# First recurrent units on the raw residual, and an earlier copy out of the first query unit

## The chip, the cores and the metric

The kernel runs on one core of one Trainium2 chip. The metric is the device time of one execution in microseconds, the median of the runs shown. Engines are named TensorE (PE; PEld is its weight load), VectorE (DVE), ScalarE (ACT), GpSimd (POOL) and SyncE (SP, which only issues DMAs). Hi and lo below are the two parts into which a float32 value is split, so that a product is made of three matmuls: hi with hi, hi with lo, lo with hi.

## The reference, cut to what matters

One inference step of a hybrid layer on 1024 prompt positions and 8 sample positions (1032 columns in all) with 1024 channels:

```python
xn = rmsnorm(x, norm_mix)
lru_x, lru_g, q, k, v = split(xn @ w_in)
xc = causal_conv(x_ext, w_conv, b_conv)          # width 4, over lru_x
hs, h_T = rg_lru(xc, ...)                        # gates, then h = a * h + u along the positions
y_lru = (hs * gelu(lru_g)) @ w_branch_lru
q = rmsnorm(q, q_gain); k = rmsnorm(k, k_gain)   # per head of 64 channels
...                                              # attention in three groups, merge, w_o, SwiGLU
```

`rmsnorm(x)` is `x * gain / rms`, with one rms for each position. So a product with the normed input is the product with `x * gain`, each column of which is multiplied by 1/rms afterwards.

## The kernel before, in words

Channels lie on the 128 partitions, in 8 tiles, and positions along the free axis, in 3 chunks of 344. A unit is the product of one 128-channel column of a weight matrix with all 8 input tiles: 3 chunks by 8 tiles by 3 matmuls, 72 matmuls, into one of two halves ("slots") of the PSUM tensor `ups`. The units come in the order of `stream` (line 160): 2 pairs of value units `v`, 8 pairs `lru` (slot 0 the recurrent input, slot 1 its gelu gate), 12 pairs `qk`, then attention and the rest. For each unit SyncE loads the weights, GpSimd splits them (`split`, lines 450 to 457: a cast, then a subtraction) once the unit before in that slot is done, TensorE multiplies, and ScalarE copies the result out of PSUM and so frees the slot (`ps_free`).

Nothing is planned by a program: each engine has its own hand-written list, and semaphores tie them. These parts bear on the change:

- *Start.* ScalarE casts each raw tile `x * gain` to its hi part (`big2`, line 882) and squares it (883). VectorE makes the lo part (1218) and adds up the squares (1222); GpSimd adds two of them (469, 472). TensorE first makes three lines of attention biases (510), which VectorE copies (1213, 1215), and then the first value pair tile by tile on the raw parts (`raw_tile`, 521). Behind its tile 7 come the sums of squares (527), the roots on ScalarE (891) and the reciprocals on VectorE (1227): 1/rms, `rinv`. The value units are scaled by it after their copy out (1232).
- *Normed input.* For tile k: VectorE multiplies by gain and `rinv` (`normed`, 1235), ScalarE casts the hi part of `big1` (910), and the lo part is made by VectorE (1240) or, for tiles 1, 4 and 7, by GpSimd (463). The first `lru` unit waits for each lo part (`normed_ready`, 569); all later units need `big1` too.
- *Recurrence.* For unit i: copy out of PSUM (`front`, 942) with the first tap of the convolution (946, 947), three more taps and three small ones on VectorE (`conv`, 1292 and 1295), two gate products on TensorE for each chunk (`gates`, 566), sigmoids on ScalarE (952, 953), gelu (960), then decay (967, 969), VectorE's squares (1303, 1304), ScalarE's root (971), VectorE's product, scan, small instructions, gelu product and its two parts (`recur`, 1303 to 1316).
- *Query and key units.* ScalarE copies a unit out, squares it and casts the squares (`evac`, 1000 to 1005); VectorE makes their lo part (`square_low`, 1334); TensorE sums the squares of each head in `aux` (`stats`, 590); ScalarE takes the root (1015), VectorE the reciprocal (1339) and the normed unit (1341), which ScalarE stores. `square_low` of the next unit stands behind 1341 in VectorE's list. TensorE runs `stats` of a unit between chunks 1 and 2 of the next one. Ahead of the first `evac` ScalarE waits until the last recurrence is over and issues two output DMAs (985 to 987).

Of the kernel before, what the change touches and what calls it, by code (L numbers as in the profile page):

```python
# [92 lines left out]
def build(nc, A, O):  # L93

    with ExitStack() as ctx:
# [36 lines left out]
        lamt = sout.rearrange("p a n -> p (a n)")[:, 0:4 * KT].rearrange("p (a n) -> p a n", a=4)  # L132
# [3 lines left out]
        sums, odd_sums, rinv = x_sq[:, 0, :], x_sq[:, 1, :], ext[:, 0, 0:NT]  # L136
        fsums, frms = ext[:, 0, 0:NT], ext[:, 3, 0:NT]
        POOL_LOW = (1, 4, 7)
# [55 lines left out]
        nf_done, nhi_done, nlo_dve, nlo_pool = sem("nf_done"), sem("nhi_done"), sem("nlo_dve"), sem("nlo_pool")  # L194
        gmix_ld, xhi_done, xlo_done, odd_done, sum_done = (sem(n) for n in ("gmix_ld", "xhi_done", "xlo_done", "odd_done", "sum_done"))
        vm_done = sem("vm_done")
# [16 lines left out]
        v_stored = two("v_stored")  # L213
# [48 lines left out]
        VO = [ext[:, 2 + j, 0:NT] for j in range(2)]  # L262
# [39 lines left out]

        def wait_low(eng, k):

            if k in POOL_LOW:
                eng.wait_ge(nlo_pool, POOL_LOW.index(k) + 1)
            else:
                eng.wait_ge(nlo_dve, k + 1 - sum(n < k for n in POOL_LOW))

# [20 lines left out]
        def _(sp):  # L330
            for name, iters, nk, src, f0, f1, step, k0 in stream:
# [57 lines left out]
                if name == "v":  # L389
                    first = 1  # L390
                    weights(0, 0)
                    for k in range(KT):
                        sp.dma_start(tmp(k), A["x_T"][k]).then_inc(x_loaded[k], 16)
                        if k == 1:
                            weights(0, 1)
                    for dst, con in consts:
                        sp.dma_start(dst, con).then_inc(const_ld, 16)
                if name == "att0":
# [3 lines left out]
                    for j in range(2):  # L402
                        sp.wait_ge(v_stored[j], 16 * 2)
# [41 lines left out]
        def _(pool):  # L445
# [13 lines left out]
            for name, iters, nk, *_ in stream:  # L459
                first = 0  # L460
                def low(k):
                    pool.wait_ge(nhi_done, k + 1)
                    nc.gpsimd.tensor_tensor(big1[:, 1, k, :], tmp(k), big1[:, 0, k, :].bitcast(F32), ALU.subtract).then_inc(nlo_pool, 1)  # L463

                if name == "v":
                    split(name, nk, 0, 0)
                    split(name, nk, 0, 1)
                    pool.wait_ge(nsq_done, 5)
                    nc.gpsimd.tensor_tensor(odd_sums, odd_sums, x_sq[:, 4, :], ALU.add).then_inc(odd_done, 1)
                    pool.wait_ge(nsq_done, 8)  # L470
                    pool.wait_ge(odd_done, 1)
                    nc.gpsimd.tensor_tensor(odd_sums, odd_sums, x_sq[:, 7, :], ALU.add).then_inc(odd_done, 1)
                    split(name, nk, 1, 0)
                    split(name, nk, 1, 1)
                    low(POOL_LOW[0])
                    continue
                if name == "lru":
                    first = 1
                    split(name, nk, 0, 0)
                    low(POOL_LOW[1])  # L480
                    low(POOL_LOW[2])
                    split(name, nk, 0, 1)
# [6 lines left out]
        def _(pe):  # L489
# [22 lines left out]
            pe.wait_ge(lines_ld, 48)  # L512
            bias_line(0)
            bias_line(1).then_inc(u_ps, 1)
            pe.wait_ge(u_sb, 1)
            bias_line(2).then_inc(u_ps, 1)

            def raw_tile(slot, k):
                for c in range(NCH):
                    for w, a in ((0, 0), (0, 1), (1, 0)):  # L520
                        ins = nc.tensor.matmul(ups[:, slot, c, 0:CH], wsp[:, slot, w, k, :], big2[:, a, k, c * CH:(c + 1) * CH],  # L521
# [8 lines left out]
            for n in range(KT + LEAD):  # L530
                if n < KT:
# [4 lines left out]
                    raw_tile(0, n)  # L536
# [9 lines left out]
                if n >= LEAD:  # L546
# [3 lines left out]
                    raw_tile(1, n - LEAD)  # L550
# [18 lines left out]
            def normed_ready(c, k):  # L569
                if c == 0:  # L570
                    wait_low(pe, k)
# [21 lines left out]
            def qk(i, first):  # L593
                for j in range(2):
                    if first and j == 0:
                        for c in range(2):
                            unit("qk", i, j, big1, parts=(c,))
                            gates(KT - 1, c + 1)
                        pe.wait_ge(gate_ev, KT * NCH + 1)
                    else:  # L600
                        unit("qk", i, j, big1, parts=(0, 1))
                    if j:
                        stats(0, i)
                    elif not first:
                        stats(1, i - 1)
# [4 lines left out]
            qk(0, True)  # L610
            with pe.Fori(1, 12) as i:
                qk(i, False)
# [242 lines left out]
        def _(act):  # L855
# [19 lines left out]
            act.dma_start(gmix[:], A["c_norm_mix"]).then_inc(gmix_ld, 16)  # L875
            act.dma_start(lines.rearrange("p (g n) -> p g n", g=NG), A["c_lines"].rearrange("g b n -> b g n")).then_inc(lines_ld, 16)
            act.dma_start(relx[0:NBK, :], A["rel_bias"]).then_inc(lines_ld, 16)
            act.dma_start(relx[NBK:NBK + 1, :], A["c_one"]).then_inc(lines_ld, 16)
            act.wait_ge(gmix_ld, 16)
            for k in range(KT):  # L880
# [3 lines left out]
                if k == 2:  # L884
                    act.wait_ge(u_sb, 2)
                    act.dma_start(u_s.rearrange("(g h) n -> h g n", g=NG), u_lines).then_inc(u_stored, 16)
            act.wait_ge(bd_zero, 1)
            gate_weights(0)
            for c in range(NCH):
# [5 lines left out]
            def values_out(n):  # L895
                i, j = n // 2, n % 2
                act.wait_ge(unit_done[j], i + (T0["v"] + 2))
                if i:
                    act.wait_ge(v_stored[j], 16)
                nc.scalar.activation(chunks(VO[j]), ups_v[j], ACT.Copy).then_inc(ps_free[j], 1)  # L900

            def values_store(n):
                j = n % 2
                act.wait_ge(vm_done, n + 1)
                nc.scalar.activation(sqkv[:, 24 + n, :], VO[j][:, SEQ:NT], ACT.Copy).then_inc(sqc_done, 1)
                act.dma_start(qkv_s[24 + n], VO[j][:, 0:SEQ]).then_inc(v_stored[j], 16)

# [8 lines left out]
            for k in range(4):  # L916
                normed_hi(k)
            values_out(2)
            for k in range(4, KT):
                normed_hi(k)  # L920
            values_store(2)

            act.wait_ge(lam_dve, 1)
            nc.scalar.activation(lamt[:, 1, :], lamt[:, 0, :], ACT.Exp, scale=-1.0).then_inc(lam_act, 1)
            act.wait_ge(lam_dve, 2)
            nc.scalar.activation(lamt[:, 3, :], lamt[:, 2, :], ACT.Ln).then_inc(lam_act, 1)


            values_out(3)
            values_store(3)  # L930
# [6 lines left out]

            def front(i):
# [4 lines left out]
                act.wait_ge(ps_free[0], i + (T0["lru"] + 2))  # L943
                act.wait_ge(u_done, i + 1)
                apart(act)
                nc.scalar.activation(XC[:, 0:SEQ], LX[:, 0:SEQ], ACT.Identity, bias=col(i, 4), scale=col(i, 0))
                nc.scalar.activation(XC[:, SEQ:NT], LX[:, SEQ + 3:NT + 3], ACT.Identity, bias=col(i, 4), scale=col(i, 3)).then_inc(xc0_done, 1)
# [25 lines left out]
            front(0)  # L973
# [702 lines left out]
```

## Time and profile before

| what | value |
|---|---|
| median of 3 runs | 2086.37 us (2084.69 to 2089.06) |
| the profiled execution's own time | 2086.76 us |
| its span, first to last instruction | 2085.0 us |
| mean granted TensorE clock | 0.988 of full speed |
| TensorE busy | 2020.2 us, 97% of the span |
| VectorE, ScalarE, GpSimd busy | 44%, 24%, 27% |

Times in the rows are microseconds from the span's start. A row of the timeline has start, duration, engine, line, instruction, output and inputs, and how many instructions in a row it merges; in brackets stands how long the engine was idle before and what released it. The ends of matmuls are modelled. A row of the waits says who waited for whom: total, how often, and the longest. L501 is a unit's matmul wherever it is called from.

### The profile page before, as it was taken

How to read it: one execution, taken by the hardware profiler on the slowest of the kernel's cores; microseconds unless marked ns; L12 is line 12 of the kernel's file. 1: busy time of each engine (PE TensorE's matmuls, PEld its weight loads, DVE VectorE, ACT ScalarE, POOL GpSimd, SP SyncE). 2: the span in 40 equal slices, each digit the busy share in tenths (PEclk: the TensorE clock that was granted, in tenths of full speed). 3: DMA queues.
4: the chain of work that ended last, by engine and by line, in shares of the span. 5: the costliest groups of instructions: out<-in, count | busy, mean ns of one | idle time of the engine just before them, and what ended most of it. 6: DMA issues, size and time to landing. Idle time of an engine off the chain costs nothing.

```text
span 2085.0 us, 32283 instructions
## 1 busy us (share of the span) xinstructions
PE 2020.2 (97%) x12884; PEld 1955.8 (94%) x12884; DVE 907.1 (44%) x913; ACT 509.4 (24%) x725; POOL 562.0 (27%) x330
## 2 busy tenths in 40 slices
PE   7899989999989999999989899999999999999999
PEld 7899988999979999999978899999999999999999
DVE  6666666767763232222256464443220333203331
ACT  4366653333334333233311012201100000000000
POOL 3433322222321111111122133233232332323322
PEclk9999999999999999999999999999999999999999
DMA  5211111222233333424377352111111111111112
GB/s 201 93 35 42 43 42 53 98 83 80 80 126 123 125 106 112 132 101 139 109 267 256 125 196 106 41 51 40 50 41 50 50 40 50 41 50 51 40 57 85
DMA packets 71594, 188.42 MB, mean 90 GB/s; under 512 B 9314, under 2 KB 28797, under 8 KB 70781
## 3 DMA queue, kind: packets, MB, share of 16 engines
q1 hardware_dynamic: 41312, 136.97, 19.3%
q10 hardware_dynamic: 30236, 50.82, 6.7%
q8 instruction: 32, 0.52, 0.1%
q14 instruction: 14, 0.11, 0.0%
HBM read 145.09 MB, written 45.81 MB: 92 GB/s over the span
## 4 chain that ended last, share of the span: by engine, by line
PE 89%; DVE 6%; ACT 1%; issue 1%; DMA 1%; POOL 1%; ACTq 0%; SPq 0%; DVEq 0%; POOLq 0%
PE ups L501 64%; PE ups L627 12%; PE ups L652 3%; PE ups L677 3%; PE aux L664 2%; PE aux L566 1%; PE aux L590 1%; PE ups L521 1%; DVE x L1339 1%; PE aux L641 0%; DVE x L1494 0%; ACT x L1085 0%; DVE ext L1227 0%; POOL big L463 0%; DVE x L1309 0%
## 5 line engine op out<-in xcount | busy, mean ns | idle before, releaser
L501 PE MATMUL ups<-big,wsp 128*128 128x344 f32 x9216 | 1482.4, 322 | 19.2 <-POOL wsp L457 8.5
L501 PEld LDWEIGHTS ups<-big,wsp 128*128 128x128 f32 x9216 | 1462.8, 189 | 35.8 <-issue 16.8
L455 POOL CAST wsp<-wraw 128x1024 fp32r<-128x1024 f32 (+2 forms) x160 | 163.6, 1022 | 1465.9 <-issue 725.2
L457 POOL TENSOR_TENSOR wsp<-wraw,wsp 128x1024 fp32r<-128x1024 f32 (+2 forms) x160 | 382.5, 2391 | 12.8
L627 PE MATMUL ups<-big,wsp 128*128 128x344 f32 x1728 | 291.8, 324 | 0.0
L627 PEld LDWEIGHTS ups<-big,wsp 128*128 128x128 f32 x1728 | 272.7, 189 | 5.3 <-issue 5.2
L1339 DVE RECIPROCAL x<-x 128x1024 f32<-128x1024 f32 x24 | 157.3, 6553 | 75.8 <-ACT x L1015 75.8
L1377 DVE SCALAR_TENSOR_TENSOR x<-ups,ext 128x256 f32<-128x256 f32 (+1 forms) x96 | 48.0, 542 | 235.8 <-PE aux L664 147.2
L1190 ACT ACTIVATE ext<-ext 128x1032 f32<-128x1032 f32 x22 | 23.5, 1068 | 482.5 <-DVE ext L1594 482.4
L1596 DVE TENSOR_TENSOR ext<-ups,ext 128x1032 f32<-128x1032 f32 x22 | 27.1, 1234 | 215.4 <-PE ups L501 215.4
L1610 DVE TENSOR_TENSOR x<-ups,x 128x1032 f32 x24 | 29.6, 1233 | 203.7 <-PE ups L501 203.7
L1085 ACT ACTIVATE x<-x,ext 128x128 f32<-128x128 f32 (+1 forms) x192 | 70.9, 440 | 60.2 <-DVE ext L1385 59.9
L1599 DVE TENSOR_TENSOR ext<-ext 128x1032 f32<-128x1032 f32 x22 | 71.1, 3233 | 4.8 <-DVE ext L1596 4.8
L1594 DVE TENSOR_TENSOR ext<-ups,ext 128x1032 f32<-128x1032 f32 x22 | 27.1, 1234 | 105.4 <-PE ups L501 105.1
L652 PE MATMUL ups<-ext 64*128 64x128 f32 (+1 forms) x384 | 67.1, 476 | 4.7 <-DVEq L1362 4.7
L677 PE MATMUL ups<-x 128*128 128x65 f32 x560 | 67.8, 270 | 0.0
L677 PEld LDWEIGHTS ups<-x 128*128 128x128 f32 x560 | 66.8, 192 | 0.0
L652 PEld LDWEIGHTS ups<-ext 64*128 64x128 f32 x384 | 43.5, 281 | 14.6 <-issue 13.1
L1015 ACT ACTIVATE x<-aux,epst 128x1024 f32<-128x1024 f32 x24 | 26.8, 1117 | 121.2 <-PE aux L590 121.2
L1390 DVE COPY x<-ups 128x260 f32<-128x260 f32 x48 | 20.4, 425 | 81.3 <-PE ups L677 81.3
L1075 ACT ACTIVATE x<-aux 128x768 f32<-128x768 f32 (+1 forms) x32 | 28.6, 892 | 82.9 <-PE ups L677 67.3
L1383 DVE TENSOR_REDUCE x<-x 128x2 f32<-128x256 f32 (+1 forms) x96 | 47.6, 539 | 1.7
(189 smaller groups left out, 1165.4 us busy)
## 6 DMA issues: line engine op xcount, KB each, us to landing
wraw<-w_in SPq DMA_DIRECT2D x52, 512.0 KB, 3.5
wraw<-w_ffn_in SPq DMA_DIRECT2D x44, 512.0 KB, 3.2
out_qkv<-x ACTq DMA_DIRECT2D x28, 512.0 KB, 2.7
ext<-out_qkv SPq DMA_DIRECT2D x24, 512.0 KB, 4.4
x<-x_T SPq DMA_DIRECT2D x16, 516.0 KB, 8.2
x<-gate_s SPq DMA_DIRECT2D x16, 516.0 KB, 4.2
wraw<-w_merge SPq DMA_DIRECT2D x16, 512.0 KB, 5.1
wraw<-w_ffn_out SPq DMA_DIRECT2D x16, 512.0 KB, 3.5
```

The lines of the kernel that those rows point to most:

```text
L455: nc.gpsimd.tensor_copy(hi, raw).then_inc(w_hi, 1)
L457: nc.gpsimd.tensor_tensor(lo, raw, hi.bitcast(F32), ALU.subtract).then_inc(w_split[slot], 1)
L501: ins = nc.tensor.matmul(ups[:, slot, c, 0:CH], wsp[:, slot, w, k, :], src[:, a, k, c * CH:(c + 1) * CH], start=(k == 0 and w + a == 0), s ...
L627: ins = nc.tensor.matmul(ups[:, 0, c, 0:CH], wsp[:, slot, w, k, :], big1[:, a2, k, c * CH:(c + 1) * CH], start=(k == 0 and w + a2 == 0), s ...
L652: ins = nc.tensor.matmul(s_bank[:, hh, 256 * m + 256 - P * nk:256 * m + 256], toks(QT, g, b)[hr], toks(KTT, g, b, nk)[hr], start=True, sto ...
L664: ins = nc.tensor.transpose(pt_bank[:, hh, c:c + P], SB[:, hh, c:c + P], ident[:])
L677: ins = nc.tensor.matmul(o_bank[:, at:at + HD + 1], PTS[:, hh, c:c + P], VTOK[:, b + 1 - nk + k, hh, :], start=(k == 0), stop=(k == nk - 1))
L1085: ins = nc.scalar.activation(SB[:, hh, cols], SB[:, hh, cols], ACT.Exp, bias=NM[:, 2 * m + hh:2 * m + hh + 1])
L1339: step.step(nc.vector.reciprocal(rms_t, rms_t))
L1377: ins = nc.vector.scalar_tensor_tensor(SB[:, :, cols], s_bank[:, :, cols], SCALE, BT[:, :, 0:P * nk][:, :, ::-1], ALU.mult, ALU.add)
L1383: ins = nc.vector.tensor_reduce(OT[:, 2 * n + m, :, HD + 1], SB[:, :, cols], AX_X, ALU.max)
L1599: step.step(nc.vector.tensor_tensor(ext[:, 1, 0:NT], ext[:, 0, 0:NT], ext[:, 1, 0:NT], ALU.mult))
```

## The change

- The first `lru` pair multiplies the raw parts in `big2`, without waiting for the normed input. At the exit VectorE multiplies both results by `rinv`, out of PSUM: the recurrent input into `LX0` in place of ScalarE's copy, the gate into `GE` ahead of the gelu. Before the second `lru` unit TensorE waits for all eight lo parts of the normed input (`nlo_done`).
- All lo parts of the normed input and all sums of squares are VectorE's; GpSimd only splits weights. The norm of tiles 6 and 7 moves behind the exit of the first unit, around its convolution. Value units 2 and 3 are scaled and stored behind the first gates.
- At the start TensorE's bias lines move between the raw tiles and are copied by ScalarE; SyncE loads the gain vector first; ScalarE runs one dummy activation early; the softplus chain of the decay constants moves ahead of the reciprocals.
- ScalarE's first `evac` waits only for the last gate product on VectorE instead of the whole recurrence; `square_low(0, 0)` goes into the last recurrence, ahead of the gelu product. The two output DMAs follow `evac(0, 0)`, still behind the recurrence's end. TensorE's first statistics move from the second to the third query unit, the next two sets to one and two chunks of the fourth; from the third pair on the order is the old one.

The core of the diff:

```diff
                 if name == "v":
                     first = 1
+                    sp.dma_start(gmix[:], A["c_norm_mix"]).then_inc(gmix_ld, 16)
                     weights(0, 0)
...
-            unit("lru", 0, 0, big1, ready=normed_ready)
-            unit("lru", 0, 1, big1)
+            unit("lru", 0, 0, big2)
+            unit("lru", 0, 1, big2)
             gates(0, 0)
+            pe.wait_ge(nlo_done, KT)
...
-            qk(0, True)
-            with pe.Fori(1, 12) as i:
-                qk(i, False)
+            for c in range(2):
+                unit("qk", 0, 0, big1, parts=(c,))
+                gates(KT - 1, c + 1)
+            unit("qk", 0, 0, big1, parts=(2,))
+            unit("qk", 0, 1, big1)
+            pe.wait_ge(gate_ev, KT * NCH + 1)
+            unit("qk", 1, 0, big1, parts=(0,))
+            stats(0, 0)
+            unit("qk", 1, 0, big1, parts=(1, 2))
+            unit("qk", 1, 1, big1, parts=(0,))
+            stats(1, 0)
+            unit("qk", 1, 1, big1, parts=(1,))
+            stats(0, 1)
+            unit("qk", 1, 1, big1, parts=(2,))
+            with pe.Fori(2, 12) as i:
+                qk(i)
...
+            act.wait_ge(ones_done, 1)
+            nc.scalar.activation(st[:, 0:1], epst[:], ACT.Identity, scale=epst[:])
             act.wait_ge(gmix_ld, 16)
...
+            act.wait_ge(const_ld, CONSTS)
+            act.wait_ge(nlo_done, 1)
+            tap(0, ext[:, 1, :])
+            for k in range(6, KT):
+                normed_hi(k)
+            act.wait_ge(nlo_done, 4)
             gate(0, 0)
+            gate(0, 1)
+            act.wait_ge(ps_free[1], T0["lru"] + 2)
+            nc.scalar.activation(GE, GE, ACT.Gelu_apprx_tanh)
+            gate(0, 2)
+            values_store(2)
+            values_store(3)
+            gate_weights(1)
+            act.wait_ge(gx_done, 1)
+            front(1)
+            decay(0)
+            gate(1, 0)
...
+            act.wait_ge(u_done, KT + 1)
+            evac(0, 0)
+            act.wait_ge(lru_done, KT)
+            act.dma_start(O["lru_out"], sout[:]).then_inc(out_done, 16)
+            act.dma_start(O["state_out"], stc[:]).then_inc(out_done, 16)
+            root(0, 0)
+            evac(0, 1)
...
                 nc.vector.tensor_copy(sout[:, ds(i, 1), 11:20], H[:, SEQ - 1:NT])
+                if last:
+                    square_low(0, 0)
                 step.step(nc.vector.tensor_tensor(U, H, GE, ALU.mult))
...
+            for k in range(6):
+                normed(k)
+                if k:
+                    normed_low(k - 1)
+            normed_low(5)
+            LX0 = ext[:, 1, :]
+            step.step(nc.vector.memset(LX0[:, 0:3], 0.0))
+            dve.wait_ge(unit_done[0], T0["lru"] + 2)
+            nc.vector.tensor_tensor(chunks(LX0[:, 3:3 + NT]), ups_v[0], chunks(rinv), ALU.mult).then_inc(ps_free[0], 1)
+            normed(6)
+            conv(0, LX0)
+            normed(7)
+            normed_low(6)
+            normed_low(7)
...
+            dve.wait_ge(unit_done[1], T0["lru"] + 2)
+            nc.vector.tensor_tensor(chunks(GE), ups_v[1], chunks(rinv), ALU.mult).then_inc(ps_free[1], 1)
+            values_scaled(2)
+            values_scaled(3)
```

## Rows read from the trace of the kernel before

**Rows 1.** The waits of TensorE, the two at the last recurrence.

```profile
PE aux L590 <- DVE ext_r L1334: 12.6, 2, 9.9
PE ups L501 <- ACT x L953: 2.7, 1, 2.7
```

**Rows 2.** TensorE's timeline, start to the first gates.

```profile
14.69 20.64 PE L521 MATMUL ups<-big,wsp 128*128 128x344 f32 x117 [1.93 <-DVE big L1218]
...
41.14 24.72 PE L501 MATMUL ups<-big,wsp 128*128 128x344 f32 x156
...
76.28 21.54 PE L501 MATMUL ups<-big,wsp 128*128 128x344 f32 x123 [2.13 <-POOL big L463]
```

**Rows 3.** TensorE's timeline, last recurrence to the third statistics.

```profile
290.36 1.32 PE L566 MATMUL aux<-x,bd 128*128 128x344 f32 x4
294.34 13.13 PE L501 MATMUL ups<-big,wsp 128*128 128x344 f32 x72 [2.67 <-ACT x L953]
317.40 2.07 PE L590 MATMUL aux<-ext_r,bones_r 128*128 128x512 f32 x4 [9.92 <-DVE ext_r L1334]
...
344.50 1.09 PE L590 MATMUL aux<-ext_r,bones_r 128*128 128x512 f32 x4
```

**Rows 4.** One microsecond: length, TensorE busy (instructions), granted clock, DMA share, GB/s.

```profile
296.00:297.00 1.00, 1.00 (x5) 0.50 0.00 0
```

**Rows 5.** Timeline of the first 17 us; one row lists line 882's instructions.

```profile
0.76 0.43 ACTq L875 DMA_DIRECT2D gmix<-c_norm_mix  x1
...
6.20 2.34 POOL L457 TENSOR_TENSOR wsp<-wraw,wsp 128x1024 fp32r<-128x1024 f32 x1
...
6.91 1.28 ACT L882 ACT_TABLE_LOAD   x1 [6.91 <-DMA x<-x_T]
...
7.55 2.73 PE L510 MATMUL aux<-big_f 33*8 33x384 f32 x4 [7.55 <-DMA big_f<-c_one]
...
9.53 1.04 POOL L455 CAST wsp<-wraw 128x1024 fp32r<-128x1024 f32 x1 [0.99 <-DMA wraw<-w_in]
...
13.27 3.68 DVE L1218 SCALAR_TENSOR_TENSOR big<-x,gmix,big 128x1032 fp32r<-128x1032 f32 x3
...
L882 ACT ACTIVATE big<-x,gmix x8: 1138/1141/1155, 8.2 to 22.2; 128x1032 fp32r<-128x1032 f32 x8
```

**Rows 6.** Timeline: VectorE and GpSimd at once, both in SBUF, and with PSUM.

```profile
58.15 3.27 POOL L457 TENSOR_TENSOR wsp<-wraw,wsp 128x1024 fp32r<-128x1024 f32 x1
59.08 3.43 DVE L1240 TENSOR_TENSOR big<-x,big 128x1032 fp32r<-128x1032 f32 x1
...
1502.42 1.04 POOL L455 CAST wsp<-wraw 128x1024 fp32r<-128x1024 f32 x1 [7.84 <-PE ups L501]
1502.42 1.23 DVE L1594 TENSOR_TENSOR ext<-ups,ext 128x1032 f32<-128x1032 f32 x1 [4.43 <-PE ups L501]
```

**Rows 7.** Timeline: tap and convolution of the first recurrent unit.

```profile
87.70 1.24 ACT L946 ACTIVATE x<-ext,par 128x1024 f32<-128x1024 f32 x1
...
89.27 4.64 DVE L1292 SCALAR_TENSOR_TENSOR x<-ext,par,x 128x1024 f32<-128x1024 f32 x3 [3.93 <-ACT x L947]
...
94.61 0.17 DVE L1299 COPY sout<-ext 128x11 f32<-128x11 f32 x1
```

**Rows 8.** Timeline of ScalarE and VectorE from the last recurrence on.

```profile
300.71 1.07 ACT L971 ACTIVATE x<-x 128x1032 f32<-128x1032 f32 x1 [1.27 <-DVE x L1304]
...
305.17 2.29 DVE L1309 TENSOR_TENSOR_SCAN x<-x 128x1024 f32<-128x1024 f32 x1
...
311.40 0.34 ACTq L986 DMA_DIRECT2D out_lru_out<-sout  x1
...
312.88 1.03 ACT L1000 ACTIVATE x<-ups 128x1032 f32<-128x1032 f32 x1 [11.11 <-issue]
...
319.51 1.11 ACT L1015 ACTIVATE x<-aux,epst 128x1024 f32<-128x1024 f32 x1 [3.32 <-PE aux L590]
...
329.54 1.21 DVE L1334 TENSOR_TENSOR ext_r<-x,ext_r 128x1024 fp32r<-128x1024 f32 x1
```

More of the change, by code:

```diff
@@ L212, in build @@
         sqc_done = sem("sqc_done")
-        v_stored = two("v_stored")
+        v_stored = [sem(f"v_stored{n}") for n in range(4)]
         bt_fill = sem("bt_fill")
@@ L591, in stats, with qk @@
                 ins.then_inc(st_done[j], 1)
-            def qk(i, first):
+            def qk(i):
                 for j in range(2):
[L595 to L605, printed above, removed]
+                    unit("qk", i, j, big1, parts=(0, 1))
+                    stats(1 - j, i - 1 + j)
                     unit("qk", i, j, big1, parts=(2,))
@@ L936, in col, with tap @@
                 return par[:, ds(i, 1), n]
+            def tap(i, lx):
+                act.wait_ge(ps_free[0], i + (T0["lru"] + 2))
+                act.wait_ge(u_done, i + 1)
+                apart(act)
+                nc.scalar.activation(XC[:, 0:SEQ], lx[:, 0:SEQ], ACT.Identity, bias=col(i, 4), scale=col(i, 0))
+                nc.scalar.activation(XC[:, SEQ:NT], lx[:, SEQ + 3:NT + 3], ACT.Identity, bias=col(i, 4), scale=col(i, 3)).then_inc(xc0_done, 1)
             def front(i):
@@ L942, in front @@
                 nc.scalar.activation(chunks(LX[:, 3:3 + NT]), ups_v[0], ACT.Copy).then_inc(ps_free[0], 1)
[L943 to L947, printed above, removed]
+                tap(i, LX)
             def gate(i, c):
@@ L1016, in root @@
                     .then_inc(rt_done[j], 1)
-            def qk(i, first):
-                if not first:
-                    root(i - 1, 1)
+            act.wait_ge(u_done, KT + 1)
[5 more added lines that the diff above has]
+            evac(0, 1)
+            with act.Fori(1, 12) as i:
+                root(i - 1, 1)
                 evac(i, 0)
-                if not first:
-                    store(i - 1, 0)
+                store(i - 1, 0)
                 root(i, 0)
                 evac(i, 1)
-                if not first:
-                    store(i - 1, 1)
-            qk(0, True)
-            with act.Fori(1, 12) as i:
-                qk(i, False)
+                store(i - 1, 1)
             root(11, 1)
@@ L1219, in _ @@
                                                ALU.mult, ALU.subtract).then_inc(xlo_done, 1)
-                if k > 1 and k not in POOL_LOW:
+                if k:
                     dve.wait_ge(nsq_done, k + 1)
-                    step.step(nc.vector.tensor_tensor(sums, sums, x_sq[:, k, :], ALU.add))
-            dve.wait_ge(odd_done, 2)
-            nc.vector.tensor_tensor(sums, sums, odd_sums, ALU.add).then_inc(sum_done, 1)
-            for c in range(NCH):
-                dve.wait_ge(nrt_done, c + 1)
-                step.step(nc.vector.reciprocal(part(rinv, c), part(rinv, c)))
```

204 lines of the change are left out of this document (84 added, 120 removed).

## The prediction, made before the changed kernel ran

> **What bounds the kernel now.** I read the busy shares first: TensorE is busy in 97% of the span, so only two things can shorten the time: TensorE's waits, and stretches in which it works at half clock. The waits by line come next, kept here to the two at the last recurrence: 9.9 us on the squares of the first query unit and 2.7 us on a sigmoid of ScalarE [rows 1]. Then TensorE's own timeline. Its 117 matmuls on the raw residual begin only at 14.69 and take 20.64 us; 156 run at 158 ns each (24.72 us); after that the first recurrent unit comes in handfuls of three, and 123 matmuls resume at 76.28 [rows 2]. 288 matmuls from 41.14 at that pace would end at 86.8; they end at 97.82. So 11.0 us are lost there. At the end of the recurrence the two waits stand inside matmul groups that are themselves stretched: 72 matmuls take 13.13 us against 11.4 [rows 3]. The clock tells why: from 296 to 297, right after the wait of 2.67 us, the granted clock is 0.50, the 1.2 GHz level, with TensorE busy [rows 4]. I count 1.7 us for each such stretch.
>
> **Part 1, the start.** Now the first cast waits for x at 6.91 and then for a table load of 1.28, and the bias lines stand ahead of everything [rows 5]. The early dummy activation takes the table load out. The gain vector's load moves ahead of weights and x on SP, so both come later by its issue of 0.4 [rows 5]; on ScalarE's queue it frees as much for the bias lines, which nobody waits for early any more. So the casts start at 7.3, and ScalarE delivers one every 2.0 us (8 from 8.2 to 22.2) [rows 5], the first at 8.45.
>
> VectorE and GpSimd exclude each other here. A 1.23 us subtraction that asked at 59.08, while GpSimd's subtraction ran to 61.42, took 3.43: it waited for the other's end. At 1502.42 a VectorE product out of PSUM and a GpSimd cast began together and both ran at full speed [rows 6]. The Trainium skill, page "SBUF — State Buffer", section "Who interferes with whom", says that an instruction with two SBUF inputs and a GpSimd one that reads SBUF block each other for the whole instruction; the rows agree. It speaks against this change, which brings VectorE's work forward into GpSimd's first two splits; without blocking the sum would be 2.1 us better.
>
> By the rows: the first split, 0.4 later, ends at 8.95, so the first low part runs 8.95 to 10.15, and TensorE starts at 10.15 instead of 14.69. The second split's cast (1.04) follows to 11.2, the second low part to 12.4, GpSimd's subtraction (2.34) to 14.75, VectorE's new second sum to 16.0, the third low part to 17.2, each VectorE step at 1.23 [rows 5]. TensorE has two tiles, 18 matmuls, 2.85 us, plus the 2.1 that its slow first matmuls cost before (20.64 against 117 times 0.158 [rows 2]): done at 15.1, idle to 17.2. Then 99 matmuls (15.65) and the three bias lines, six instructions at about 0.34 (four took 2.73 on an engine that had just begun [rows 5], and I take half; 2.05 in all): 34.9, where it was 35.33. **Gain 0.4.** Bounds: 2.5 if the blocking does not starve it; a loss of 1.3 if the pause adds a half-clock stretch. I take the middle, since the blocking is what the nearest rows show. The two sums that move from GpSimd to VectorE are in these steps. Casting the bias lines on ScalarE, softplus before the reciprocals and the later store of the bias rows hide behind TensorE's 13 tiles; uncovered they would cost some 1 to 3 us.
>
> **Part 2, the first recurrent units.** They read what the value units read, so TensorE runs 288 matmuls from 40.7 without a wait and reaches the gates at 86.35 instead of 97.82, and ends their 1.3 us [rows 3] at 87.65. Behind that stands a new wait: all eight low parts of the normed input, with the whole of the next unit queued behind it on TensorE. The first unit ends at 40.7 + 34.25 = 74.95. VectorE scales it out of PSUM (1.23 [rows 6], not blocked) to 76.2. ScalarE's tap takes 1.57 (87.70 to 89.27 [rows 7]): 77.8. Meanwhile the norm of tile 6 asked at 76.2 and is blocked by the split of 75.0 to 78.45: done 79.7. The convolution took 5.3, of which 0.9 was a block [rows 7]: 84.1, before the gates need it. Norm of tile 7, low part 6: 86.6. The split that the second unit's end at 86.35 releases puts its cast in between (87.7), then low part 7: 88.9. **TensorE waits 1.3 us.** Bounds: nothing if VectorE goes first and the splits come late, 2.5 if the subtraction too gets in front. Three low parts moved from GpSimd cost VectorE 3.7, hidden: by the same steps it is through with tiles 0 to 5 near 71 and then idles until 74.95. The second unit's scaling, the two value products and the four gate-weight DMAs, ahead of ScalarE's next copy out, have until that unit's end near 102 to be done; they come to less than 6 us after the gates. Sum of both parts: the next unit starts at 88.9 instead of 99.1: **10.2 us.**
>
> **Part 3, the last recurrence** (clock of the run before). TensorE no longer waits at 291.67 [rows 3]: 24 matmuls to 295.5, 72 to 306.9, 24 to 310.7; there the first statistics stand now. The copy out is behind ScalarE's root at 300.71 [rows 8] and takes 4.5 less 1.2 (312.88 to 317.40 [rows 3, 8]), so it is done by 306. VectorE's scan ends near 306.2 (2.29 [rows 8]; the split that blocks the product ahead of it has moved to 295.5). The inserted subtraction asks at 306.9, just as the second query unit releases a split: cast to 307.9, subtraction to 309.1, on time for 310.7. But what follows it, a product and two copies, 3.2 us (3.9 from the scan's end to the next output DMA [rows 8], less 0.7 that I count for four small instructions), then meets GpSimd's subtraction and ends at 314.7, 3.3 later than before (311.40 [rows 8]). ScalarE waits for exactly that before its two output DMAs (about 0.9) and the first root, 315.6. From root to the next low part took 11.24, of which 0.9 was a block [rows 8]: 10.4 free, so 326.0. TensorE is there at 323.1, waits 2.9, and the third statistics follow after only 24 matmuls: ready 327.0 + 10.5 = 337.5, TensorE there at 330.9, **a wait of 6.6 us that is new**. Before they ran at 344.50 [rows 3]. 7.0 earlier, less a half-clock stretch as after the old 9.9 us wait (1.0 on the statistics, 1.7 on 72 matmuls [rows 3]): **4.3 us gained**. Bounds: 9.5 if VectorE is not blocked and the clock holds; nothing if two more blocks of 2 us fall into the chain.
>
> **Sum.** 10.2 + 4.3 = 14.5 us off the profiled execution's 2086.76 (span 2085.0), 2072.3. The median of the runs is 0.4 lower, so 2071.9. After the third statistics the order of work is the old one, so the rest only moves forward; the later store of values 2 and 3 has until the attention.
>
> **Rivals.** *The waits stay short* (0.25): blocking falls the other way in all three places: 2.1 + 1.3 + 5.2 more, 2063.3. For: whoever asks first wins, and the instants are within 0.1 us. Against: GpSimd's 3.4 us must be served somewhere.
> *Each short wait also costs half clock* (0.12): the pauses of 2.1 and 1.3 each bring a stretch of 1.7, 2075.3, and up to 2077.5 with the longer one. For: rows 4 after 2.67 us. Against: these waits are shorter. The Trainium skill, page "TensorE: Matmul & The Clock Gate", section "HAM oscillation — how this bites in real kernels", describes waits between groups that leave each next group cold.
> *The early copy buys nothing* (0.08): the statistics of the query loop are a chain through root, reciprocal and subtraction; with two more blocks the third set still runs at 344.50. Only part 2 is left: 2076.2, with the second rival's half clocks 2079.6.
> *The change does not do it* (0.03): some wait of mine on the first units is a longer one, the normed input then being late by the whole 10 us; within 0.2%.
> *Slower* (0.03): in the query loop the chain has 12.3 us per unit (11.4 of matmuls, about 0.9 of statistics) and uses 10.4. If the shifted start put GpSimd's subtraction on the product and subtraction after the reciprocal, instead of under the reciprocal, chain 10.4 + 2.3 plus the blocked copy 0.6 would be 13.3: 22 statistics, each 1 us late, 22 us against 14.5: 2094. It decides from a chain of 12.3 on. Against: splits follow unit ends, and these keep their places in the loop.
> My forecast itself holds 0.49.
>
> **How the numbers follow.** The low end, 2063.0, takes in the first rival; the high end, 2078.5, the second and half of the third. About 0.2% (4 us) is what a measurement of this kernel can tell from no change: faster 0.94, same 0.03, slower 0.03.
>
> **What would show it.** Right: the raw matmuls start near 10 with one pause of about 2 us; no handfuls of three; TensorE waits once, about 1 us, for a low part after the gates; no 2.7 us wait at the last recurrence; the 9.9 us wait is replaced by one near 3 and one near 7, and the clock falls once there. Wrong: a statistics wait over 10 us, waits that recur through the query loop, or a TensorE that still waits for the normed input for more than 4 us.

## The result, and the profile after

The changed kernel takes 2072.47 us in the median (2071.17 to 2074.35, 4 runs) against 2086.28 of the kernel before on the same chip (2084.69 to 2089.06): a ratio of 0.9934, 95% interval 0.9918 to 0.9949. That is **13.8 us faster**; forecast were 14.5 and 2071.9 us. Its profiled execution took 2071.17 us (span 2069.4, granted clock 0.993); TensorE is busy for 2014.0 us, still 97% of the span.

First the waits of TensorE, in the columns of [rows 1]. L472 is now a unit's matmul, L486 a raw tile's, L559 the statistics.

```profile
PE aux L559 <- DVE ext_r L1270: 12.2, 3, 6.5
```

The 2.7 us wait of [rows 1] is gone and the 9.9 us one is in pieces. A wait of 1.6 us for the last low part is new. The total for statistics is almost the old one (12.2 against 12.6, with one of 2.7 in each that stands at the end of the query loop). Gone too are two rows of the kernel before, in which TensorE waited for the normed input of the first recurrent unit:

```profile
PE ups L501 <- POOL big L463: 4.6, 2, 2.5
...
PE ups L501 <- DVE big L1240: 2.6, 2, 1.5
```

TensorE's busy time is shorter as well, 2014.0 us against 2020.2, for the same work: fewer of its matmuls run at half clock.

The start of the changed kernel, timeline rows of TensorE, VectorE and GpSimd, to be read against [rows 2, 5]:

```profile
10.13 5.30 PE L486 MATMUL ups<-big,wsp 128*128 128x344 f32 x18 [10.13 <-DVE big L1205]
...
11.24 3.25 POOL L450 TENSOR_TENSOR wsp<-wraw,wsp 128x1024 fp32r<-128x1024 f32 x1
...
12.17 3.41 DVE L1209 TENSOR_TENSOR big_f<-big_f 128x1032 f32<-128x1032 f32 x1
...
15.61 1.29 DVE L1205 SCALAR_TENSOR_TENSOR big<-x,gmix,big 128x1032 fp32r<-128x1032 f32 x1
...
16.96 1.69 PE L486 MATMUL ups<-big,wsp 128*128 128x344 f32 x9 [1.53 <-DVE big L1205]
...
41.12 45.50 PE L472 MATMUL ups<-big,wsp 128*128 128x344 f32 x288
```

TensorE starts on the raw tiles 4.6 us earlier than in [rows 2] and then stands for 1.5 us. VectorE's sum (3.41 us here, 1.22 when alone at 16.82) began under GpSimd's split, and the third low part is behind it. The second value pair starts at 41.12; in [rows 2] it was 41.14. The start gained nothing: besides the pause, the 4.6 us went to the bias lines, which ran ahead of 14.69 before (2.1), and to slower groups (0.9).

Then the first recurrent units, in place of [rows 2, 7]; the last row is the next unit in the kernel before:

```profile
75.40 1.23 DVE L1305 TENSOR_TENSOR ext<-ups,ext 128x1032 f32<-128x1032 f32 x1 [8.04 <-PE ups L472]
...
76.55 3.52 DVE L1242 SCALAR_TENSOR_TENSOR x<-x,gmix,ext 128x1032 f32<-128x1032 f32 x1
76.58 2.40 POOL L450 TENSOR_TENSOR wsp<-wraw,wsp 128x1024 fp32r<-128x1024 f32 x1
...
85.89 3.22 DVE L1246 TENSOR_TENSOR big<-x,big 128x1032 fp32r<-128x1032 f32 x2
...
86.46 1.32 PE L538 MATMUL aux<-x,bd 128*128 128x344 f32 x4
86.78 1.23 POOL L448 CAST wsp<-wraw 128x1024 fp32r<-128x1024 f32 x1 [7.80 <-issue]
...
89.43 4.04 PE L472 MATMUL ups<-big,wsp 128*128 128x344 f32 x24 [1.65 <-DVE big L1246]
...
98.55 4.20 PE L501 MATMUL ups<-big,wsp 128*128 128x344 f32 x24
```

The gates come at 86.46 instead of 97.66. Behind them TensorE waits 1.65 us for the last low part. VectorE idled for 8.04 us before 75.40 and then had six steps to do in a row, two of them blocked by GpSimd: the norm (3.52 instead of 1.29) and one of the two low parts (3.22 for both). The next unit starts at 89.43; before it was 98.55. That is 9.1 us. The 288 matmuls reach the gates 11.2 us sooner: 7.2 us are the waits that are gone, and 4.0 are matmuls that ran slowly behind them (in the kernel before the granted clock was 0.50 from 71 to 80). The rest of the difference is the new wait and a gap of 0.4 between gates and unit.

And the last recurrence, in place of [rows 3, 8]; the last row is the fourth set of statistics in the kernel before:

```profile
297.55 1.22 DVE L1270 TENSOR_TENSOR ext_r<-x,ext_r 128x1024 fp32r<-128x1024 f32 x1
297.66 2.01 POOL L448 CAST wsp<-wraw 128x1024 fp32r<-128x1024 f32 x1 [7.80 <-issue]
298.69 2.07 DVE L1286 TENSOR_TENSOR x<-x 128x1032 f32<-128x1032 f32 x1
299.75 3.26 POOL L450 TENSOR_TENSOR wsp<-wraw,wsp 128x1024 fp32r<-128x1024 f32 x1
300.91 2.65 DVE L1288 CAST big<-x 128x1032 fp32r<-128x1032 f32 x1
...
301.11 1.09 PE L559 MATMUL aux<-ext_r,bones_r 128*128 128x512 f32 x4
...
306.12 1.12 ACT L1006 ACTIVATE x<-aux,epst 128x1024 f32<-128x1024 f32 x1 [9.60 <-issue]
...
316.54 1.20 PE L559 MATMUL aux<-ext_r,bones_r 128*128 128x512 f32 x4 [3.01 <-DVE ext_r L1270]
...
317.57 3.93 PE L472 MATMUL ups<-big,wsp 128*128 128x344 f32 x24
...
327.98 2.07 PE L559 MATMUL aux<-ext_r,bones_r 128*128 128x512 f32 x4 [6.48 <-DVE ext_r L1270]
329.86 12.70 PE L472 MATMUL ups<-big,wsp 128*128 128x344 f32 x72
342.40 1.09 PE L559 MATMUL aux<-ext_r,bones_r 128*128 128x512 f32 x4
...
356.75 1.09 PE L590 MATMUL aux<-ext_r,bones_r 128*128 128x512 f32 x4
```

120 matmuls now run from 281.97 without a wait, and the first statistics follow at 301.11 without one. The second set waits 3.01 us and the third 6.48. Behind the third the clock falls, as in [rows 4] (length, then busy time with instructions of TensorE, its weight load, VectorE, ScalarE and GpSimd, granted clock, DMA share, GB/s):

```profile
317.00:318.00 1.00, 1.00 (x7) 0.86 (x6) 0.00 (x0) 0.23 (x1) 0.00 (x0) 1.00 0.00 0
...
328.00:329.00 1.00, 1.00 (x2) 0.81 (x3) 0.00 (x0) 0.00 (x0) 0.00 (x0) 0.50 0.00 0
```

After 3.01 us of waiting the granted clock was 1.00, the 2.4 GHz level; after 6.48 it was 0.50. The third statistics run 16.5 us earlier than in [rows 3]: 9.1 from the first units and 7.4 here. The half clock gives 2.2 of it back (statistics 2.07 instead of 1.09, the next 72 matmuls 12.70 instead of 11.49), so the fourth set comes at 342.40 instead of 356.75, 14.35 us earlier. The spans differ by 15.6; most of the rest is in later waits for split weights, 8.5 us in all before and 6.6 after, the longest 4.9 and 3.1.

### The profile page after: what moved, and what is told of

Read it like the earlier page. It is cut to its first block, busy times and chain, and to the rows that moved or that the text cites. A ratio compares the mean times of both kernels' runs of the same rounds, so it can differ in the third digit from the quotient of the medians.

```text
span 2069.4 us, 32282 instructions
## 1 busy us (share of the span) xinstructions
PE 2014.0 (97%) x12884; PEld 1952.3 (94%) x12884; DVE 905.9 (44%) x919; ACT 509.3 (25%) x726; POOL 552.1 (27%) x325
## 4 chain that ended last, share of the span: by engine, by line
PE 89%; DVE 6%; ACT 1%; issue 1%; DMA 1%; POOL 0%; ACTq 0%; SPq 0%; DVEq 0%; POOLq 0%
PE ups L472 64%; PE ups L600 13%; PE ups L625 3%; PE ups L650 3%; PE aux L637 2%; DVE x L1335 1%; PE aux L538 1%; PE aux L559 1%; PE ups L486 1%; PE aux L614 0%; DVE x L1489 0%; DVE x L1259 0%; DMA x<-o_s 0%; DVE x L1280 0%; ACT x L1076 0%
## 5 line engine op out<-in xcount | busy, mean ns | idle before, releaser
L472 PE MATMUL ups<-big,wsp 128*128 128x344 f32 x9216 | 1477.3, 321 | 9.1 <-POOL wsp L450 6.6
L472 PEld LDWEIGHTS ups<-big,wsp 128*128 128x128 f32 x9216 | 1459.4, 189 | 24.0 <-issue 16.9
L448 POOL CAST wsp<-wraw 128x1024 fp32r<-128x1024 f32 (+2 forms) x160 | 167.8, 1049 | 1485.0 <-issue 724.0
L1006 ACT ACTIVATE x<-aux,epst 128x1024 f32<-128x1024 f32 x24 | 26.8, 1117 | 132.5 <-PE aux L559 122.9
```

The costliest lines, as they stand in the source:

```text
L448: nc.gpsimd.tensor_copy(hi, raw).then_inc(w_hi, 1)
```

## The experiments

Each kernel was timed beside the kernel before on the same chip; its medians there were 2086.72 (for the first four), 2086.59 (for the next four) and 2086.04 us (for the last two). The runs of one kernel scatter by 3 to 8 us, so an edit worth 1 or 2 us is read from the rows.

**The first units alone.** The changed kernel with its query part put back (TensorE's old order of statistics too, not shown):

```diff
-            act.wait_ge(u_done, KT + 1)
-            evac(0, 0)
             act.wait_ge(lru_done, KT)
...
-                if last:
-                    square_low(0, 0)
...
+            square_low(0, 0)
```

> The changed kernel with the query part undone: old order of statistics, copy out and lo part of the first query unit behind the whole recurrence. Theory (the two parts are independent): the second recurrent unit still starts at 89.4 against 98.55 before, 9.1 us early, and stays so; the waits of 2.7 and 9.9 us at the last recurrence come back with their half-clock stretches; 2086.3 - 9.1 = 2077.2 us. Rival (the 9 us are partly lent: the earlier recurrence only waits longer somewhere else): one of the two returning waits is longer than before, and the time is 2080 us or more.

Measured: 2077.4 us, ratio 0.9947 (0.9931 to 0.9962). Both old waits are back in TensorE's timeline, and there is something at the start that the changed kernel's profile does not have:

```profile
17.64 2.46 PE L486 MATMUL ups<-big,wsp 128*128 128x344 f32 x9 [1.93 <-DVE big L1204]
...
22.68 8.55 PE L486 MATMUL ups<-big,wsp 128*128 128x344 f32 x36
...
290.41 13.13 PE L472 MATMUL ups<-big,wsp 128*128 128x344 f32 x72 [2.67 <-ACT x L927]
...
312.92 2.08 PE L559 MATMUL aux<-ext_r,bones_r 128*128 128x512 f32 x4 [9.38 <-DVE ext_r L1269]
```

After a pause of 1.93 us the granted clock falls to 0.50 from 19 to 28: the last of the 9 matmuls, four bias instructions (2.73 us instead of 1.45) and about half of the 36 run at half pace (8.55 us against 5.91 in the changed kernel are 2.64 more, 17 matmuls at 0.158 extra). The second value pair starts at 46.48, 5.4 us later than in the changed kernel, 4.7 of them by the half pace, the others by a later start and the longer pause. So in this execution, the longest of four (2079.16 us), the second rival came true at the start, and the next recurrent unit starts at 94.79, not at 89.4. But from the second value pair to that unit it takes 48.31 us, as long as in the changed kernel and 9.1 less than before (57.41): this stage's gain does not hang on the query part.

**The query part alone**, on the kernel before:

```diff
-            act.wait_ge(lru_done, KT)
...
+            act.wait_ge(u_done, KT + 1)
+            evac(0, 0)
+            act.wait_ge(lru_done, KT)
...
+                if last:
+                    square_low(0, 0)
...
-            square_low(0, 0)
```

> The kernel before with the query part alone: new order of statistics, early copy out and lo part, nothing of the start and of the first recurrent units. Theory: third statistics 16.5 - 9.1 = 7.4 us earlier than 344.50, so at 337.1, then a half-clock stretch that leaves 5.2 us; 2081.1 us. Rival (the query part needs the first part, or buys nothing by itself): no gain over 2 us, 2084 us or more.

Measured: 2079.99 us, ratio 0.9964 (0.9951 to 0.9977). Its second and third statistics, from TensorE's timeline:

```profile
326.13 1.61 PE L590 MATMUL aux<-ext_r,bones_r 128*128 128x512 f32 x4 [2.93 <-DVE ext_r L1305]
327.53 5.11 PE L501 MATMUL ups<-big,wsp 128*128 128x344 f32 x24
337.98 2.07 PE L590 MATMUL aux<-ext_r,bones_r 128*128 128x512 f32 x4 [5.34 <-DVE ext_r L1305]
```

The same two new waits, without any change at the start. Here the shorter one cost half clock as well: 24 matmuls in 5.11 us, 3.93 in the changed kernel. The fourth set (352.97) comes 3.8 us earlier than before, not 5.2: this execution started 0.4 late, and half pace cost 1.0 more. It was also the longest of five (2085.38). By the medians the parts bring 9.3 and 6.7 us alone, together 13.8: they add up within the scatter.

**The last norms early.** VectorE makes all eight norms before it scales the first unit, in the 8 us in which it idled:

```diff
-            for k in range(6):
+            for k in range(KT):
                 normed(k)
...
-            normed_low(5)
+            normed_low(KT - 1)
...
-            normed(6)
             conv(0, LX0)
-            normed(7)
-            normed_low(6)
-            normed_low(7)
```

> The changed kernel with the norm, the casts and the lo parts of tiles 6 and 7 moved ahead of the first recurrent unit's exit, where VectorE is idle for 8 us. Theory (TensorE's wait of 1.65 us for the lo part of tile 7 is only a matter of VectorE's order): the wait is gone, nothing takes its place, all later work comes 1.65 us earlier; 2070.8 us. Rival (VectorE is short of time there, the split in between blocks it and the exit itself comes late): TensorE waits at the first gates instead, and the time stays at 2072.5 us.

Measured: 2069.38 us, ratio 0.9912 (0.9899 to 0.9926). The row behind the first gates, at 87.05, is now

```profile
87.94 4.20 PE L472 MATMUL ups<-big,wsp 128*128 128x344 f32 x24
```

with no wait in front of it, and no new one elsewhere. So the 1.65 us came from the place of the last two norms in VectorE's list, and from nothing else. At the fourth statistics (342.01) only 0.4 us of it are left in this execution: it started 0.6 late, and its 24 matmuls behind the second statistics ran at half pace (5.19 us).

**The sums one tile later**, so that the third low part does not queue behind a blocked sum:

```diff
-                if k:
-                    dve.wait_ge(nsq_done, k + 1)
-                    ins = nc.vector.tensor_tensor(sums, sums, x_sq[:, k, :], ALU.add)
...
+                if k > 1:
+                    dve.wait_ge(nsq_done, k)
+                    step.step(nc.vector.tensor_tensor(sums, sums, x_sq[:, k - 1, :], ALU.add))
```

> The changed kernel with each sum of squares one tile later in VectorE's list, so that the third lo part no longer stands behind a sum that GpSimd's split blocks. Theory (the pause of 1.5 us at the start is that sum, blocked by GpSimd's second split): the third lo part ends near 15.6 instead of 16.9, the pause shrinks to about 0.2 us, the second value pair starts near 39.8 instead of 41.12; 2071.2 us. Rival (TensorE's pace at the start has another bound behind it, ScalarE's casts at 2.0 us or the bias lines): the pause moves to a later tile and the second value pair still starts at 41.1; 2072.5 us.

Measured: 2070.88 us, ratio 0.9919 (0.9905 to 0.9932). The first three tiles run in one piece:

```profile
10.49 7.24 PE L486 MATMUL ups<-big,wsp 128*128 128x344 f32 x27 [10.49 <-DVE big L1205]
```

The second value pair starts at 40.21, 0.9 us earlier (1.3 expected; TensorE began 0.4 later here), and the next recurrent unit at 88.51 with its wait of 1.65 as before: the gain passes through.

**The first root earlier.** ScalarE takes it before it waits for the recurrence's end:

```diff
             evac(0, 0)
+            root(0, 0)
             act.wait_ge(lru_done, KT)
+            evac(0, 1)
             act.dma_start(O["lru_out"], sout[:]).then_inc(out_done, 16)
             act.dma_start(O["state_out"], stc[:]).then_inc(out_done, 16)
-            root(0, 0)
-            evac(0, 1)
```

> The changed kernel with ScalarE's wait for the end of the recurrence and its two output DMAs moved behind the first root (the wait ahead of the second copy out, the DMAs behind it). Theory (the 3.0 us wait at the second statistics is that wait: the root runs at 306.12 although its statistics ended at 302.2, and VectorE's reciprocal could start when VectorE is through at 304.9): reciprocal 304.9 instead of 307.27, the second statistics wait 0.6 us instead of 3.0, the third set, 11.4 us behind, comes 2.4 us earlier and waits 6.5 as now; 2070.1 us. Rival (the chain at that place is bound by the second unit's copy out, which also stands behind the recurrence): second and third statistics stay where they are; 2072.5 us.

Measured: 2073.12 us, ratio 0.993 (0.9917 to 0.9944): no gain that can be seen. Its timeline of ScalarE, VectorE, GpSimd and TensorE shows why:

```profile
307.18 1.12 ACT L1006 ACTIVATE x<-aux,epst 128x1024 f32<-128x1024 f32 x1 [5.72 <-PE aux L559]
...
310.09 6.55 DVE L1335 RECIPROCAL x<-x 128x1024 f32<-128x1024 f32 x1 [0.32 <-DVE big L1289]
...
315.99 2.38 POOL L450 TENSOR_TENSOR wsp<-wraw,wsp 128x1024 fp32r<-128x1024 f32 x1
316.89 2.56 DVE L1337 SCALAR_TENSOR_TENSOR x<-x,gqk 128x1024 f32<-128x1024 f32 x1 [0.24 <-DVE x L1335]
...
320.64 1.37 PE L559 MATMUL aux<-ext_r,bones_r 128*128 128x512 f32 x4 [2.17 <-DVE ext_r L1270]
```

The root comes 1.1 us after the first statistics instead of 5.0, but VectorE is in the recurrence until 309.8 and starts the reciprocal only 2.1 us sooner; then the product behind it falls on GpSimd's split (2.56 us; 1.29 in the changed kernel, where the reciprocal covers the split). The second statistics come 14.59 us after the first instead of 15.43: 0.8 of the expected 2.4. Besides, this execution had a pause of 2.01 us at the start and half pace behind it: its second value pair starts at 46.10.

**TensorE kept at work.** 34 spare matmuls ahead of the third statistics; their results are overwritten:

```diff
+            for n in range(34):
+                nc.tensor.matmul(ups[:, 1, 2, 0:CH], wsp[:, 1, 0, n % KT, :], big1[:, 0, n % KT, 2 * CH:3 * CH], start=True, stop=True)
             stats(0, 1)
```

> The changed kernel with 34 spare matmuls ahead of the third statistics, into the PSUM bank that the next chunk overwrites: some 5.4 us of work inside the wait of 6.5. Theory (that wait costs 6.5 us and then 2.2 to 2.8 us more, because the clock falls): the third statistics start at the same time after the second, take 1.09 instead of 2.07, the 72 matmuls behind take 11.5 instead of 12.7, the granted clock stays at 1.0; 2.2 us less, 2070.3 us. Rival (the slow stretch costs nothing, since the statistics behind it would wait for VectorE anyway): the fourth statistics now wait 2 us; 2072.5 us.

Measured: 2071.94 us, ratio 0.9932 (0.9919 to 0.9946). TensorE's timeline at the second and third statistics:

```profile
316.46 2.08 PE L559 MATMUL aux<-ext_r,bones_r 128*128 128x512 f32 x4 [2.96 <-DVE ext_r L1272]
318.33 4.50 PE L472 MATMUL ups<-big,wsp 128*128 128x344 f32 x24
...
328.78 1.19 PE L559 MATMUL aux<-ext_r,bones_r 128*128 128x512 f32 x4 [0.55 <-DVE ext_r L1272]
329.81 11.49 PE L472 MATMUL ups<-big,wsp 128*128 128x344 f32 x72
```

Third statistics of 1.19 and 72 matmuls at full pace: with the wait filled, the half clock behind it is gone. Here, though, the second wait brought half pace, which it did not in the changed kernel's profile, and that pushed the third set back by 0.8. The fourth set (341.14) is 1.3 us earlier, not 2.2.

**The bias lines into the pause**, one tile earlier:

```diff
-                if n == 2:
+                if n == 1:
                     pe.wait_ge(lines_ld, 48)
```

> The changed kernel with the first two bias lines (1.4 us of TensorE) ahead of the third raw tile instead of behind it. Theory (the start's pause of 1.5 us is idle time of TensorE that other work can fill): the pause is gone, the second value pair starts near 39.8 instead of 41.12, and the start no longer falls to half clock behind the pause as it did in the profile of the units alone (46.48); 2071.1 us. Rival (the bias lines are not what follows on the path): the same 41.1, 2072.5 us.

Measured: 2070.45 us, ratio 0.9919 (0.9905 to 0.9932). The bias lines run from 15.40, the pause is gone, and the second value pair starts at 39.44, 1.7 us earlier; the next recurrent unit at 87.73.

**Four edits together**: norms early, sums late, root first, 34 spare matmuls.

> All at once: early norms, late sums, root first, spare matmuls. Theory (four separate places on TensorE's path, so the gains add): 1.65 + 1.3 + 2.4 + 2.2 = 7.5 us, 2065.0 us. Rival (they share one path, as the recurrence and the query chain do): less than 5 us, 2067.5 us or more.

Measured: 2067.02 us (2064.91 to 2069.18), ratio 0.9904 (0.9889 to 0.9919). The second value pair starts at 39.84, the next recurrent unit at 86.08 without a wait, the fourth statistics at 337.18, 5.2 us earlier than in the changed kernel. That lies between the theory (7.5 us, 2065.0) and its rival (under 5, 2067.5 or more). 2.17 us of waiting at the second statistics are left, with half pace behind them again:

```profile
312.51 2.07 PE L559 MATMUL aux<-ext_r,bones_r 128*128 128x512 f32 x4 [2.17 <-DVE ext_r L1269]
314.38 4.58 PE L472 MATMUL ups<-big,wsp 128*128 128x344 f32 x24
```

**That wait filled as well**, with 13 spare matmuls:

```diff
+            for n in range(13):
+                nc.tensor.matmul(ups[:, 1, 1, 0:CH], wsp[:, 1, 0, n % KT, :], big1[:, 0, n % KT, CH:2 * CH], start=True, stop=True)
             stats(1, 0)
```

> The four edits together, plus 13 spare matmuls (their results are overwritten by the next real group, so that they only use time) right ahead of the second statistics, where TensorE still waited 2.17 us with the four edits. Theory (waits cost twice, once in idle time and once in half clock): the 13 spare matmuls last about 2.05 us and fill the wait; the second statistics, at 2.07 us with the wait in front of them, take 1.1, and the 24 matmuls behind them 3.8 instead of 4.58. The statistics are not any earlier, what follows gains 1.7 us, and 34 spare ones behind it become partly too many or are filled into the next wait: the fourth statistics come some 24 us after the second, against 24.67. Time: about 1 us less than with the four edits, near 2066. Rival (the clock does not hang on these waits): the second statistics still take 2.07, and the time stays at 2067.0 or above, the spare matmuls being pure cost.

Measured: 2066.6 us (2064.78 to 2069.05), ratio 0.9908 (0.9895 to 0.9922).

```profile
312.87 1.19 PE L559 MATMUL aux<-ext_r,bones_r 128*128 128x512 f32 x4
313.90 3.93 PE L472 MATMUL ups<-big,wsp 128*128 128x344 f32 x24
```

The statistics and the 24 matmuls are at full pace, and the fourth set comes 23.8 us after the second (24.67 without the edit): as expected in the rows. The 0.4 us between the medians can't be told from nothing. These two are the fastest versions measured, some 20 us below the kernel before.

**A longer pause at the start.** The third raw tile waits for the fourth low part:

```diff
-                    pe.wait_ge(xlo_done, n + 1)
+                    pe.wait_ge(xlo_done, 4 if n == 2 else n + 1)
```

> The changed kernel, with one edit: TensorE's third raw tile waits for the fourth low part instead of the third, so that the pause of 1.5 us at the start becomes one of about 4 us (the third low part was done at 16.9, the fourth is due about 2.4 us later). Theory A (the length of the pause decides whether the matmuls behind it run at half pace: 1.1 to 1.6 us did not bring it, 1.93 and 2.01 us did): in the profile the matmuls behind the pause run at half pace, 36 in about 8.5 us instead of 5.91, the second value pair starts near 46 to 48 instead of 41.12, and the median comes 5 to 7 us above the changed kernel's 2072.5, 2077 to 2079. Theory B (it is chance, the pause's length does not matter): half pace in some executions only, and the median is above by no more than what the later fourth tile costs, 1 to 2.5 us: 2073 to 2075, with a spread of 5 us between the runs.

Measured: 2077.57 us (2074.8 to 2078.93), ratio 0.9959 (0.9945 to 0.9972).

```profile
19.85 2.95 PE L486 MATMUL ups<-big,wsp 128*128 128x344 f32 x9 [3.85 <-DVE big L1205]
...
24.25 5.91 PE L486 MATMUL ups<-big,wsp 128*128 128x344 f32 x36
```

The median lies where theory A has it, the profiled execution does not: its half pace lasted for 9 matmuls (2.95 us, 1.69 in the changed kernel), its second value pair starts at 45.41. Of the 4.3 us that this is late, 2.9 are the later third tile (theory B had 1 to 2.5) and 1.4 the half pace. It was the second shortest of five runs; what the others did here was not seen, so the median does not decide between the theories. Over all profiles with a pause at this place: none of half pace after 1.06, 1.53 and 1.61 us, some after 1.93, 2.01 and 3.85. In these six the length of the pause goes with whether half pace follows; how long it then lasts (some 3 to 10 us) it does not set. Six profiles are few, the edges are not known, and one wait of 2.69 us late in the query loop went both ways (last section).

## Why the prediction was right

**Part 1, the start: gain 0.4 forecast, 0.0 measured.** The steps held: first cast 7.50 (7.3 forecast), TensorE from 10.13 (10.15), a sum blocked by the split, third low part done at 16.90 (17.2). The term that was mis-sized is the pace: I priced 99 matmuls at 0.158 us each, 15.65 in all; in their three groups (16.96 to 18.58, 19.96 to 25.80, 26.54 to 35.15) they took 16.07. The bias lines cost 2.12 in place of 2.05. And 0.2 of the forecast gain came from the old end, 35.33, which is a modelled end: what follows starts at 35.16 in both kernels within 0.01 us.

**Part 2: 10.2 forecast with part 1, 9.1 measured.** Every step from the first unit's end to the low part of tile 7 came within 0.7 us, in the forecast order, with both blocks (ScalarE's tap, 0.9 late, is not on this path); the wait is 1.65 instead of 1.3. Two terms were off by 0.5 each. The next unit starts at 89.43 instead of 88.9. And the old start was set at 99.1, by adding 1.3 for gates to the end of a matmul group; the modelled ends overlap, and the row of before stands at 98.55. The rule behind it (a VectorE instruction with two inputs in SBUF and one of GpSimd exclude each other) held wherever it was used; the reciprocal of 307.27, with one input, took its 6.55 us beside a cast and a subtraction of GpSimd. The Trainium skill, page "SBUF — State Buffer", section "Who interferes with whom", has also casts on the list of those that can take the shared port, and the trace agrees: the cast of 300.91 took 2.65 us, the other seven of its line 0.70, while the product out of PSUM at 75.40 took its 1.23 beside GpSimd's cast.

**Part 3: 7.0 forecast less 2.7, measured 7.4 less 2.2.** On the clock of the run before (9.1 added) the recurrence's end shows at 314.0 (the output DMA at 304.92; 314.7 forecast), the root at 315.2 (315.6), the second low part at 325.6 (326.0); the waits are 3.01 and 6.48 (2.9 and 6.6). The block fell one step later than forecast: the inserted subtraction ran free at 1.22, the product and the cast behind it were blocked. One half-clock stretch, after the long wait, as forecast.

**The sum:** 9.1 + 5.2 = 14.3 at the fourth statistics, against 14.5. That they agree so well is in part luck: the first two parts fell 1.1 us short, and the third brought 0.9 more than forecast. Some 1.2 us more came later in the span, most of it in waits for split weights, which the prediction had left out; the median moved by 13.8.

**The rivals.** *The waits stay short* fell: the split was served ahead of VectorE in all three places. *Each short wait also costs half clock* was nearer than its 0.12 says. The pause at the start cost clock in two of the five profiles that had it as the change makes it (and in the one in which it was lengthened), though not in the changed kernel's; the 1.65 us wait after the gates cost none (24 matmuls in 4.04). And the wait at the second statistics, to which I gave no half clock, brought half pace in eight of the nine profiles that had it, all but the changed kernel's own. It costs little there: the slow matmuls run into the third wait, which shrinks (5.26 in place of 6.48 with the norms early), so that the statistics themselves, up to 1 us longer, push the chain, and the half pace behind the third wait, which lasts longer in some (72 matmuls in up to 13.34 us). From the second to the fourth statistics these profiles without spare matmuls took 25.3 to 26.8 us, the changed kernel 25.9. The Trainium skill's page "TensorE: Matmul & The Clock Gate", section "HAM oscillation — how this bites in real kernels", tells of waits that leave every next group cold; the traces agree for the third wait wherever it was not filled, and for the second one in all profiles but one. *The early copy buys nothing* fell with the query part alone, and *the change does not do it* with the first units alone. *Slower* did not come: the reciprocal covers the split in the loop. With the root first one such product did fall on a split, at 1.3 us.

## What to carry to other kernels

An engine that runs at 97% gains by having its order changed so that it never waits for what is made late; but look at what the freed time then releases, since a wait that is broken up comes back in pieces behind the engine that is next. Where two engines block each other, work that is moved into a hole of one lands on the other's turn: place it where nobody waits for it (the norms, which GpSimd blocks in the early place too, one low part there to 3.44 us; the sums, behind the low part), and price it blocked. A short wait is worth filling with useful work, since behind it the clock may fall. Spare matmuls took the half clock away too, but moved what follows by 1.3 us at most, which the medians do not show. For edits of 1 or 2 us compare rows, not single times.

## What the runs showed that I had not expected

- **One wait, two outcomes.** The wait at the second statistics was followed by 24 matmuls in 3.93 us in the changed kernel (3.01 us waited), and in the other profiles by 24 in 4.50 (2.96) to 5.86 (2.91); two of 2.17 by 4.58 and 5.36. The last wait for statistics, at the end of the query loop, is 2.69 or 2.70 us long in all twelve profiles: behind it 24 matmuls took 3.93 or 3.94 us in eight of them and 4.98 to 5.41 in four. The changed kernel, and behind it the one with late sums:

```profile
586.68 1.20 PE L559 MATMUL aux<-ext_r,bones_r 128*128 128x512 f32 x4 [2.69 <-DVE ext_r L1270]
587.71 3.93 PE L600 MATMUL ups<-big,wsp 128*128 128x344 f32 x24
...
585.13 1.31 PE L559 MATMUL aux<-ext_r,bones_r 128*128 128x512 f32 x4 [2.70 <-DVE ext_r L1268]
586.24 5.40 PE L600 MATMUL ups<-big,wsp 128*128 128x344 f32 x24
```

Its length does not by itself say what comes after, and one profile shows one of the outcomes.
- **The pause at the start can cost more than itself:** 4.7 us behind one of 1.93, by half pace over some 10 us.
- **Taking something off the chain moved it onto a lock:** the root 3.9 us sooner gave 0.8.
